# One add per residual pair moved from the vector engine to GpSimd, in a decoder layer on one core

## The reference

```
x = x + 0.5 * rmsnorm(swiglu_ffn(rmsnorm(x, ffn1_pre_g), ...), ffn1_post_g)     # post1
x = x + rmsnorm(mixer(rmsnorm(x, mix_pre_g), ...), mix_post_g)                  # post2
x = x + 0.5 * rmsnorm(swiglu_ffn(rmsnorm(x, ffn2_pre_g), ...), ffn2_post_g)     # post3
x = x + rmsnorm(sigmoid(rmsnorm(x, ple_norm_g) @ ple_w_gate) * (p @ ple_w_proj),
                ple_post_g)                                                     # post4
```

## Time and profile before

| | us |
|---|---|
| median of 3 runs (lowest, highest) | 2338.41 (2334.86, 2341.21) |
| span of the profiled execution | 2337.7 |
| PE busy in the span | 2158.0 (92%) |
| DVE busy | 1317.6 (56%) |
| ACT busy | 769.8 (33%) |
| POOL busy | 0.9 |

### The profile page before, as it was taken

How to read it: one execution, slowest core, us unless ns; L and a number is a source line. 1 busy time by engine, 2 the same in 40 slices (tenths; PEclk the granted TensorE clock), 3 DMA queues, 4 the chain that set the end, 5 groups by cost and what they waited for, 6 DMA issues and landing times. The chain is left out here.

```text
span 2337.7 us, 34611 instructions
## 1 busy us (share of the span) xinstructions
PE 2158.0 (92%) x13020; PEld 2106.1 (90%) x13020; DVE 1317.6 (56%) x2620; ACT 769.8 (33%) x1500; POOL 0.9 (0%) x8
## 2 busy tenths in 40 slices
PE   5899999999999878999989689999999999995886
PEld 5899999999999878887789689999999999995886
DVE  4544444543445666988555764545434554557686
ACT  4311121221122333365575532212221121225563
POOL 0000000000000000000000000000000000000000
PEclk8999999999999889999999889999999999998897
DMA  4101111101111011100014201111101111102222
GB/s 149 37 28 45 54 54 54 54 27 35 45 54 54 1 45 41 46 1 19 19 38 144 91 1 55 55 54 54 45 18 45 54 54 54 54 1 73 72 91 75
DMA packets 92360, 116.15 MB, mean 50 GB/s; under 512 B 4596, under 2 KB 83704, under 8 KB 92282
## 3 DMA queue, kind: packets, MB, share of 16 engines
q1 hardware_dynamic: 91065, 110.79, 14.4%
q10 hardware_dynamic: 1216, 4.33, 0.6%
HBM read 110.15 MB, written 4.95 MB: 49 GB/s over the span
## 5 line engine op out<-in xcount | busy, mean ns | idle before, releaser
L589 PE MATMUL ps<-x_hi,w_lo 128*128 128x352 f32 x2688 | 883.2, 329 | 17.8 <-DVE w_lo L1503 8.8
L590 PE MATMUL ps<-x_lo,w_hi 128*128 128x352 f32 x2688 | 872.9, 325 | 0.0
L591 PE MATMUL ps<-x_hi,w_hi 128*128 128x352 f32 x2688 | 871.9, 324 | 0.0
L589 PEld LDWEIGHTS ps<-x_hi,w_lo 128*128 128x128 f32 x2688 | 514.6, 191 | 19.1 <-DVE w_lo L1503 9.5
L590 PEld LDWEIGHTS ps<-x_lo,w_hi 128*128 128x128 f32 x2688 | 515.3, 192 | 0.0
L591 PEld LDWEIGHTS ps<-x_hi,w_hi 128*128 128x128 f32 x2688 | 513.5, 191 | 0.0
L589 PE MATMUL ps<-a_hi,wd_lo 128*128 128x352 f32 x1104 | 361.6, 328 | 24.6 <-DVE a_lo L1600 11.6
L590 PE MATMUL ps<-a_lo,wd_hi 128*128 128x352 f32 x1104 | 357.7, 324 | 0.0
L591 PE MATMUL ps<-a_hi,wd_hi 128*128 128x352 f32 x1104 | 357.3, 324 | 0.0
L1650 DVE TENSOR_TENSOR acc<-ps,acc 128x352 f32<-128x352 f32 x480 | 249.3, 523 | 88.7 <-PE ps L591 82.8
L1583 DVE TENSOR_TENSOR tmp_u<-ps,rstd_pre 128x352 f32<-128x352 f32 x132 | 69.1, 524 | 370.7 <-PE ps L591 370.7
(11 more groups left out here) (172 smaller groups left out, 1678.2 us busy)
## 6 DMA issues: line engine op xcount, KB each, us to landing
raw<-in_ffn_w_gu_dram SPq DMA_DIRECT2D x88, 512.0 KB, 3.5
rawd<-in_ffn_w_down_dram SPq DMA_DIRECT2D x22, 1024.0 KB, 7.6
raw<-in_w_out_dram SPq DMA_DIRECT2D x24, 512.0 KB, 3.5
raw<-in_ple_w_gate_dram SPq DMA_DIRECT2D x24, 512.0 KB, 3.4
raw<-in_w_in_dram SPq DMA_DIRECT2D x16, 512.0 KB, 4.0
x_in<-in_x_prompt_dram ACTq DMA_DIRECT2D x6, 512.0 KB, 7.8
out_dram<-y_stage SPq DMA_DIRECT2D x6, 512.0 KB, 2.8
rawd<-in_ple_w_proj_dram SPq DMA_DIRECT2D x1, 1024.0 KB, 7.2
```

The costliest lines, as they stand in the source:

```text
L589: eng.matmul(dst, wl, xh, start=first, stop=False)
L590: eng.matmul(dst, wh, xl, start=False, stop=False)
L591: return eng.matmul(dst, wh, xh, start=False, stop=last)
```

## The change

GpSimd gets a queue of 48 adds. For each seam and each chunk it waits until PE has done the last product that reads this chunk of the residual, and then adds `x_hi` and `x_lo` pair by pair into `x_full`, which lies at the address of `x_lo` as plain fp32. Each add raises a new semaphore `x_sum`. In `apply_pair` DVE waits for `x_sum` and adds `x_full` in the two instructions that added `x_hi`; the add of `x_lo` over the pair is gone, and the second of the two instructions signals `x_new` or `y_fin`.

```
-        x_lo = tile("x_lo", [P, KT, TOK], F32R)
+        x_lo, x_lo_at, _ = place("x_lo", [P, KT, TOK], F32R)
+        x_full = place("x_full", [P, KT, TOK], offset=x_lo_at)[0]
...
+        x_sum = sem("x_sum")
...
+            def restore(c, last_product):
+
+                eng.wait_ge(psum_full, last_product)
+                for q in range(PAIRS):
+                    sl = slice(2 * q, 2 * q + 2)
+                    eng.tensor_tensor(x_full[:, sl, cols(c)], f32(x_hi[:, sl, cols(c)]),
+                                      f32(x_lo[:, sl, cols(c)]), ALU.add).then_inc(x_sum, 1)
+
+            for seam in range(4):
+                for c in range(NC):
+                    if seam in (0, 2):
+                        restore(c, (NI - 1) * STEP + gate_at(seam // 2, NI - 1, c) + 4)
+                    elif seam == 1:
+                        restore(c, RING["in", 7, c, 1] + 1)
+                    else:
+                        restore(c, RING["ple", c, 3, 1] + 1)
...
                 r, m, two = rstd(post, c), 2 * q, src(c, 2 * q, 2)
+                seam = ("post1", "post2", "post3", "post4").index(post)
                 n = mark(eng.tensor_tensor(two, two, r.unsqueeze(1).broadcast_to([P, 2, C]),
                                            ALU.mult))
                 eng.wait_ge(dve_own, n)
+                eng.wait_ge(x_sum, PAIRS * (NC * seam + c) + q + 1)
                 for h in range(2):
                     t = src(c, m + h)[:, 0, :]
-                    n = mark(eng.scalar_tensor_tensor(t, t, gain(m + h),
-                                                      f32(x_hi[:, m + h, cols(c)]),
-                                                      ALU.mult, ALU.add))
-                eng.wait_ge(dve_own, n)
-                eng.tensor_tensor(two, two, f32(x_lo[:, m:m + 2, cols(c)]), ALU.add
-                                  ).then_inc(x_new if pre else y_fin, 1)
+                    ins = eng.scalar_tensor_tensor(t, t, gain(m + h), x_full[:, m + h, cols(c)],
+                                                   ALU.mult, ALU.add)
+                ins.then_inc(x_new if pre else y_fin, 1)
```

## The result

| | before | after |
|---|---|---|
| median of 4 runs (lowest, highest), us | 2339.81 (2334.86, 2341.41) | 2363.41 (2361.82, 2370.23) |
| span of the profiled execution, us | 2337.7 | 2362.1 |

The change makes the kernel slower by 1.0%: ratio 1.0104, interval 1.0084 to 1.0124. The time lies outside the predicted range and on the other side of no change. It is 4 us from the first rival's 2367.

The account below looks back on a forecast made before the run. PE was taken to bound the FFN steps and DVE the seams. Span 2337.7 - 38.6 (gain) + 15.2 (instructions held up) = 2314.3 us, with 0.7 from span to median 2315.0; range 2298 to 2358.

Parts of the forecast that it names:

- the first rival: Turn-taking: GpSimd's adds and DVE's two-input instructions exclude each other through each whole burst; 63 us, time 2367, chance 0.30.
- the price of the bursts: Each chunk's four GpSimd adds, a burst, hold up one DVE instruction by 1.27 us; 15.2 us for twelve bursts.
- The gain on DVE's side: Removing 48 pair instructions in four seams gives 34.6 us on the path plus 4 from the clock, 38.6 us.
- the clock's share: Three PE stops of about 6.1 us shrink, avoiding the low clock behind them; nothing to 8 us, taken as 4.
- The terms by stops: The gain seam by seam at PE's stops: post1 10.4, post2 7.4, post3 8.6, post4 8.2, together 34.6 us.
- Small terms: A GpSimd add takes 1.7 us; `x_sum` late or ACT limiting a seam was a rival near 2335, chance 0.02.
- The weighing: Chances for the whole kernel: faster by over 0.3% 0.54, within 0.3% 0.15, slower 0.31.
- The rival's own break-even: Turn-taking decides from about 3.2 us a burst on, two of four adds; chance 0.30.
- the chain it named: The a_hi/a_lo chain behind each chunk's last products, where PE waits and DVE has no spare time.

Follow-up runs that it names:

- Experiment 2: The changed kernel, but DVE keeps one instruction per pair, a maximum of the pair with itself, which changes no value; ratio 1.0263 to the kernel before.
- experiments 6 and 7: The changed kernel with eleven of twelve bursts started later, ratio 0.9900 to before; then also two badly chosen places mended, chunk 2's last burst using its own buffer, 0.9855.
- experiment 4: The changed kernel, but GpSimd writes zeros to x_full and reads nothing, leaving the residual out; ratio 0.9826 to the kernel before.
- experiment 1: The changed kernel without GpSimd adds, DVE adding x_hi only, the residual's low part left out; ratio 0.9826 to the kernel before, span 2305.8 us.
- experiment 3: The changed kernel, but GpSimd copies x_hi into x_full instead of adding, leaving the low part out; ratio 0.9884 to the kernel before.

## Why the prediction was wrong, step by step

**The step that failed** is the price of the bursts: "I take one instruction held up in each burst, since only the first GpSimd add meets a DVE that has been idle". It stood in the sum with 15.2 us. The runs show 56.3 us by spans (2362.1 less 2305.8) and 65 by ratios (a profile is one execution, the ratio is one of several runs), and all four instructions held up in every FFN burst (7.37 to 7.40 us for the four in each of the six, 2.04 before). The reason given was wrong in this: which engine had been idle matters for the first meeting only. After it both queues are full, and the two engines alternate one for one, as the timeline of the first burst shows. Experiment 2 shows the cost without the gain, experiments 6 and 7 show most of it vanish when the same adds are placed elsewhere, and experiment 4 shows that GpSimd must read for it.

**The first rival's sizes** hold fairly well. It had 38 us for six FFN bursts; the stops grew by 5.3 each, 32. That is the chain itself: the four DVE instructions took 2.04 us before (758.83 to 760.87) and take 7.38 now (757.88 to 765.26), 5.34 more, and the stop grew by 5.34. With halved adds they take 4.42, 2.38 more, and the stop 2.38; with copies 3.76, 1.72 more, and the stop 1.72. Where the two engines alternate, a DVE instruction costs GpSimd's pitch, the time between the ends of two of its instructions: 1.91 us an add of 704 (759.16 to 764.88 is 5.72 for three), 1.17 an add of 352 (759.99 to 763.49, 3.50 for three), 1.01 a copy of 704 (758.14 to 761.16, 3.03 for three). For the mixer it had 13; against experiment 1 the stop at 1205.77 is 6.1 longer and those of the next chunk (2.18 and 5.79 against 1.73) 6.2. For ple it had 12; 1.1 (at 2261.41), 6.4 (at 2277.66) and 3.5 (8.55 against 5.09) make 11.0. Together 55.4. Not all of it reaches the end: part of the third burst's cost is hidden in the stop at the sums behind it (7.17 in place of 9.01), and in post3 a stop of 1.72 us for a down sum, at 2130.10 in experiment 1, is gone. That leaves 51.8, and by the pages' spans and busy times PE is idle for 51.9 us more than in experiment 1 (197.8 against 145.9). The other 4.4 of the 56.3 are PE being busy for longer (2164.3 against 2159.9), and the clock is seen to take part of them: behind the stop of 7.91 at 799.26 the granted clock is 0.50, the lower level of 1.2 GHz, for 2 us and 0.69 for the next 2, where behind experiment 1's stop of 2.57 at 789.38 it is 1.00. From that stop to the sums behind it takes 20.0 us (799.26 to 819.26) in place of 18.5.

**The gain on DVE's side was right, the clock's share was not shown.** Forecast 34.6 and 4 for the clock, 38.6; experiment 1 has 40.7 by ratio and 31.9 by span. By the pages PE is idle for 33.8 us less than before (145.9 against 179.7), close to the 34.6. But it is busy for 1.9 us more, where the clock was to give back 4: behind the shorter stop at 807.88 the same 168 PE instructions up to the next stop are busy for 28.33 us in place of 29.83, but the mixer's 1494 take 288.21 in place of 286.09, at a granted clock of 0.96 in place of 0.97. The terms by stops, before less experiment 1: chunk 0 of post1 3.2 (forecast 3.0); chunk 1 2.8 and 1.0 at the stop in front of it (3.7); chunk 2 3.7 (3.7); chunks of post2 2.7, 2.9 and 1.8, 7.4 in all (7.4); ple's 1.91 at 2240.23 gone (1.9); from the sums at 2309.84 to the end 27.9 us become 22.3 (from 2283.51), 5.6 less (5.5). After has the shorter stops too, at 819.26 and 895.95 above. A pair's successor starts 1.00 us behind its first L1581 (806.29 and 805.29), as forecast.

**Small terms right:** a GpSimd add alone takes 1.66 us (1.7 forecast, with some luck, since its upper bound put one input at 1.16 and experiment 3's first copy takes 0.77); no wait of DVE is put down to GpSimd, so `x_sum` is never late; ACT is busy for 770.2 us in place of 769.8 and doesn't become a limit.

**The weighing** was wrong, too. No row of before could show the two engines together, and with nothing for or against it, taking a value near the lower end gave "faster" 0.54. The rival's own break-even, 3.2 us a burst, meant that two adds of four decided, and the chain it named had no slack at all. The Trainium skill, SBUF — State Buffer, Who interferes with whom, states the exclusion as the runs have it: two-input vector instructions held by reading GpSimd instructions (experiments 2 and 3), not by writing ones (experiment 4), and vector instructions with at most one SBUF input, outside the engine's two-port modes, free of it (here those that read PSUM, 526 ns at most). A stated rule that names just this pair of operations deserved more than 0.30.

## What to carry to other kernels

Moving an operation whose inputs lie in SBUF to GpSimd doesn't by itself take it off DVE's path: beside a queue of two-input DVE instructions, each GpSimd instruction cost DVE most of its own duration (1.47 us for an add of 704, the pitch of 1.91 less DVE's own 0.44, where the pair saved 0.93). Ask of such a move when it runs, not only whether it is done in time; started as soon as its data are ready it met PE's tightest chain, and placed where DVE idles or reads PSUM the same 48 adds turned 1.0% slower into 1.45% faster. Left where they were and only halved in size, the adds cost 0.3% in place of 1.0%.

## What the runs showed of the hardware that was not expected

- The two engines alternate strictly, one instruction each, for as long as both have work: the four adds of an FFN burst take 7.39 us in place of 6.64, the four DVE instructions 7.38 in place of 2.04. GpSimd loses 0.75 us in this, DVE 5.3.
- A held-up DVE instruction has no idle time before it. It is recorded as a long one, about 2.0 us in place of 0.52, which raised DVE's busy time while its work became less.
- A GpSimd copy with one input holds DVE as an add does, only for its own shorter duration: a pitch of 1.01 us for copies of 128x704 beside DVE, against 1.91 for adds.
